# The mixing stage written anew: S5 over four tokens with stacked taps, feature-major q and k, masks and sums by TensorE products, a new order of units

## The reference, cut to what matters

```python
dq, dk, dv, mq, mk, mv, mo, mi, mf, su = split_columns(x @ w_in, IN_WIDTHS)
# differential attention, 4 heads, two maps each, chunk-causal (chunks of 64 tokens)
s = einsum('bqhmd,bkhmd->bhmqk', rope(dq), rope(dk)) * scale
p = softmax(where(allowed, s, -inf)); a = p[:, :, 0] - lam * p[:, :, 1]
a_out = rms_norm(einsum('bhqk,bkhe->bqhe', a, dv), diff_norm_g)
# mLSTM, 4 heads: scores times exp(log_d - m_t), causal, after a 4-tap convolution
qk = silu(causal_conv(concat(mq, mk)))
b_out = sigmoid(mo) * rms_norm(mlstm(q, k, v, gates))
# S5: 16 groups of 16 channels, each a diagonal complex state of 64
x_t = lam_bar * x_(t-1) + b_bar u_t;  y = gelu(Re(C x) + D u);  y = y * sigmoid(y @ glu_w + b)
return concat(a_out, b_out, y) @ w_out
```

## Time and profile before

| what | value |
| --- | --- |
| median of 3 runs | 1377.72 us (1377.54 to 1380.18) |
| profiled execution | 1376.7 us |
| its span, first to last instruction | 1374.9 us |
| mean granted clock of PE | 0.959 of full speed |
| PE busy | 1264.1 us, 92% of the span |
| DVE, ACT, POOL busy | 59%, 42%, 14% |
| data moved | 219.52 MB, mean 160 GB/s |

### The profile page before, as it was taken

How to read it: one execution, slowest core, us unless ns; L and a number is a source line. 1 busy time by engine, 2 the same in 40 slices (tenths; PEclk the granted TensorE clock), 3 DMA queues, 4 the chain that set the end, 5 groups by cost and what they waited for, 6 DMA issues and landing times.

```text
span 1374.9 us, 15895 instructions
## 1 busy us (share of the span) xinstructions
PE 1264.1 (92%) x6568; PEld 1068.6 (78%) x6568; DVE 812.4 (59%) x1130; ACT 578.1 (42%) x656; POOL 192.8 (14%) x181
## 2 busy tenths in 40 slices
...
GB/s 282 236 184 184 184 184 163 144 123 123 31 92 158 128 204 184 184 188 192 192 148 270 186 184 184 184 151 156 92 61 62 139 118 143 152 184 186 190 193 43
DMA packets 155911, 219.52 MB, mean 160 GB/s; under 512 B 6816, under 2 KB 127776, under 8 KB 155840
## 3 DMA queue, kind: packets, MB, share of 16 engines
...
## 4 chain that ended last, share of the span: by engine, by line
PE 65%; issue 16%; DVE 11%; ACT 3%; POOL 2%; DMA 1%; SPq 0%; DVEq 0%; POOLq 0%
PE PS L469 20%; PE PS L470 19%; PE PS L471 19%; DVE WL L1376 3%; ACT WH L1043 1%; PE PS L500 1%; DMA RAW<-in_ffn_w_up 1%; DVE COUT L1560 1%; DVE ZS L1548 1%; PE PS L964 1%; PE PS L988 1%; ACT XH L1043 1%; PE PS L537 1%; POOL RO L1997 1%; ACT PR L1160 1%
## 5 line engine op out<-in xcount | busy, mean ns | idle before, releaser
L1376 DVE TENSOR_TENSOR WL<-RAW,WH 128x2048 fp32r<-128x2048 f32 (+1 forms) x198 | 445.3, 2253 | 272.4 <-ACT WH L1043 272.3
L1043 ACT ACTIVATE WH<-RAW 128x2048 fp32r<-128x2048 f32 (+1 forms) x198 | 370.5, 1877 | 148.4 <-DMA RAW<-in_ffn_w_up 128.5
L469 PE MATMUL PS<-WH,XH 128*128 128x512 f32 x832 | 333.4, 401 | 24.6 <-DVE WL L1376 9.4
L470 PE MATMUL PS<-WL,XH 128*128 128x512 f32 x832 | 327.5, 394 | 0.0
L471 PE MATMUL PS<-WH,XL 128*128 128x512 f32 x832 | 327.0, 393 | 0.0
L469 PEld LDWEIGHTS PS<-WH,XH 128*128 128x128 f32 x832 | 158.2, 190 | 59.0 <-DVE WL L1376 9.9
L471 PEld LDWEIGHTS PS<-WH,XL 128*128 128x128 f32 x832 | 158.2, 190 | 33.8
L470 PEld LDWEIGHTS PS<-WL,XH 128*128 128x128 f32 x832 | 158.4, 190 | 31.0
L469 PE MATMUL PS<-WH,HH 128*128 128x512 f32 x352 | 138.6, 394 | 5.7 <-issue 5.7
L470 PE MATMUL PS<-WL,HH 128*128 128x512 f32 x352 | 137.6, 391 | 0.0
L471 PE MATMUL PS<-WH,HL 128*128 128x512 f32 x352 | 137.6, 391 | 0.0
...
## 6 DMA issues: line engine op xcount, KB each, us to landing
...
```

The costliest lines, as they stand in the source:

```text
L469: nc.tensor.matmul(out_ap, sh, mh, start=first, stop=False)
L470: nc.tensor.matmul(out_ap, sh, ml, start=False, stop=False)
L1043: return nc.scalar.activation(dst, src, ACT.Copy)
L1376: return v.tensor_tensor(dst, full, hi.bitcast(F32), ALU.subtract)
```

## The change

The mixing stage computes the same outputs in another way.

- S5 takes four tokens a step (64 steps). `s5_gather` puts the four taps of u on partitions beside each other, so that `s5_in` is 16 products of 64 columns inside unit `MQ`, `s5_local` 8 and `s5_out` twice 8; `s5_scatter` spreads the result again. DVE makes the states alone (`s5_states`, two calls); POOL has no part in it. In the FFN before it, `scale_c` on POOL is 49 instructions for 25, `s5_turn` is three calls for one, `s5_taps` is 16 products of 128 columns in two halves, and ACT and DVE copy and add more pieces.
- q and k are projected feature-major. RoPE is a copy on ACT, one PE product of 512 columns with a permutation (`swap_halves`, four a layer) and three DVE operations; the turns and POOL's part go.
- The chunk mask is added in PSUM by a product over one row for each score block; the causal mask of the mLSTM decay by products with `tri` in `spread`; ACT then takes exp from PSUM with a bias. `decay_args` and the masking on DVE go.
- Both maps are exponentiated, turned (six turns a head for three) and multiplied by v with a column of ones, which gives the sums; they are combined behind that product. RMS roots go to POOL as a power. One convolution tap moves from DVE to ACT; the gate scaling moves from POOL to DVE.
- The order of units and of all four programs is new. Three fillers of layer 0 stand between the heads, one between `W3` and `W4`.

The core of the diff (the programs of `mix` for PE, then the start of DVE's, without most of their waits):

```diff
-        order += [(l, "DQ", 0), (l, "DQ", 1), (l, "SU", 0), (l, "MQ", 0), (l, "MK", 0), (l, "DK", 0), (l, "DK", 1),
-                  (l, "DV", 0), (l, "DV", 1), (l, "MM", 0), (l, "MM", 1)]
-        order += FILL["mid", l]
-        order += [(l, "W", i) for i in range(5)]
+        order += [(l, "DV", 0), (l, "DV", 1), (l, "DQ", 0), (l, "DK", 0), (l, "SU", 0), (l, "MQ", 0), (l, "MK", 0),
+                  (l, "DQ", 1), (l, "DK", 1), (l, "MM", 0), (l, "MM", 1)]
+        mid = FILL["mid", l]
+        order += mid[0:3] + [(l, "W", i) for i in range(4)] + mid[3:4] + [(l, "W", 4)]
         order += FILL["xattn", l]
...
+def s5_gather(l):
+    pe.wait_ge(ut_ready.sem, ut_ready.at(l, 1))
+    for tap in range(TAPS):
+        r = 32 * tap
+        out_ap = PS[r:r + 32, 5, :].rearrange("p (f j k) -> p j f k", f=2, j=BANDS)
+        for j in range(BANDS):
+            mm = nc.tensor.matmul(out_ap[:, j], ident[:, 32 * j:32 * j + 32],
+                                  UT[:, :, tap * STEPS:tap * STEPS + STEPS], start=True, stop=True)
+    mm.then_inc(u4_done.sem, 1)
...
+def s5_in(l):
+    pe.wait_ge(u4_ready.sem, u4_ready.at(l, 1))
+    for i in range(TILES):
         for part in range(2):
...
+            o = part * 256 + (i % 4) * STEPS
+            mm = nc.tensor.matmul(PS[:, 4 + i // 4, o:o + STEPS], PB[:, i, part, :], U4[:, i, :],
+                                  start=True, stop=True)
+        if i % 4 == 3:
+            mm.then_inc(bu_done.sem, 1)
...
 def s5_local(l):
     pe.wait_ge(km_ready.sem, km_ready.at(l, 1))
...
+    for i in range(TILES):
+        mm = nc.tensor.matmul(PS[:, 2, i * STEPS:i * STEPS + STEPS], KM[:, i, :], U4[:, i, :],
+                              start=(i == 0), stop=False, skip_group_check=True)
+    mm.then_inc(km_used.sem, 1)
...
+def s5_out(l, b):
+    pe.wait_ge(state_ready.sem, state_ready.at(l, b + 1))
+    if b == 0:
         pe.wait_ge(cp_ready.sem, cp_ready.at(l, 1))
...
+    for i in range(4 * b, 4 * b + 4):
+        o = i * STEPS
+        for part in range(2):
+            mm = nc.tensor.matmul(PS[:, 2, o + 1:o + STEPS],
+                                  CQ[:, part, i, 1:TAPS + 1, :].rearrange("p a c -> p (a c)"),
+                                  ZW[:, b, part, (i % 4) * STEPS:(i % 4) * STEPS + STEPS - 1],
+                                  start=False, stop=True, skip_group_check=True)
     mm.then_inc(state_used.sem, 1)
...
+def s5_scatter(l):
+    pe.wait_ge(gelu_done.sem, gelu_done.at(l, 1))
+    g = U4[:, :, :].rearrange("p (f j) k -> p j f k", f=2)
+    for j in range(BANDS):
+        out_ap = PS[32 * j:32 * j + 32, 2, :].rearrange("p (f a k) -> p a f k", f=2, a=TAPS)
+        for tap in range(TAPS):
+            mm = nc.tensor.matmul(out_ap[:, tap], ident[:, 32 * tap:32 * tap + 32], g[:, j],
+                                  start=True, stop=True)
+    mm.then_inc(g4_done.sem, 1)
...
+def swap_halves(l, i):
+    b = (0, 1, 3, 3)[i]
+    pe.wait_ge(swap_in.sem, swap_in.at(l, i + 1))
...
+    nc.tensor.matmul(bank(b), kst[:, K_SWAP:K_SWAP + P], XE[:, :, :].rearrange("p h n -> p (h n)"),
+                     start=True, stop=True).then_inc(swap_done.sem, 1)
...
+def diff_scores(l, h):
+    b = head_bank(h)
+    pe.wait_ge(roped.sem, roped.at(l, 2 if h == 0 else 4))
+    if h >= 2:
+        pe.wait_ge(do_read.sem, do_read.at(l, h - 1))
+    u = h // 2
+    for q0, q1, k1 in ((0, P, P), (P, SEQ, SEQ)):
+        for m in range(2):
+            r = 64 * m
+            nc.tensor.matmul(PS[:, b + m, q0:q0 + k1], DQT[r:r + 64, u, h % 2, q0:q1],
+                             DKT[r:r + 64, u, h % 2, 0:k1], start=True, stop=False,
+                             skip_group_check=True)
+            mm = nc.tensor.matmul(PS[:, b + m, q0 + k1 - 64:q0 + k1], kst[r:r + 1, K_EARLY:K_EARLY + P],
+                                  kst[r:r + 1, K_FAR:K_FAR + 64], start=False, stop=True,
+                                  skip_group_check=True)
+    mm.then_inc(ds_done.sem, 1)
...
 def diff_out(l, h):
+    b = head_bank(h)
     pe.wait_ge(daT_read.sem, daT_read.at(l, h + 1))
...
+    for m in range(2):
+        nc.tensor.matmul(PS[:, b + m, 0:129], AT[:, m, 0:P], DV[:, 0, h, :], start=True, stop=True)
+        nc.tensor.matmul(PS[:, b + m, 129:258], AT[:, m, P:2 * P], DV[:, 0, h, :], start=True, stop=False)
+        mm = nc.tensor.matmul(PS[:, b + m, 129:258], AT[:, m, 2 * P:3 * P], DV[:, 1, h, :],
+                              start=False, stop=True)
+    mm.then_inc(do_done.sem, 1)
...
+def spread(l):
+    pe.wait_ge(cols_read.sem, cols_read.at(l, 1))
+    for i in range(2):
+        for hh in range(2):
+            h = 2 * i + hh
+            pick = ident[0:4, h:h + 1].to_broadcast([4, P])
+            nc.tensor.matmul(PS[:, i, hh * SEQ:hh * SEQ + SEQ], pick, R_MAX, start=True, stop=False,
+                             skip_group_check=True)
+            nc.tensor.matmul(PS[:, i, hh * SEQ:hh * SEQ + P], ident, tri, start=False, stop=True,
+                             skip_group_check=True)
+            nc.tensor.matmul(PS[:, 3, h * P:h * P + P], pick, R_MAX[:, P:SEQ], start=True, stop=False)
+            mm = nc.tensor.matmul(PS[:, 3, h * P:h * P + P], ident, tri, start=False, stop=True)
+        mm.then_inc(mbc_done.sem, 1)
...
+    form_b(UNIT[l, "DQ", 0], 6, XH, XL)
+    form_b_around(UNIT[l, "DK", 0], 7, lambda: swap_halves(l, 0))
+    form_b_around(UNIT[l, "SU", 0], 2, lambda: swap_halves(l, 1))
...
+    s5_gather(l)
...
+    form_b_around(UNIT[l, "MQ", 0], 0, lambda: s5_in(l))
...
+    diff_scores(l, 0)
     s5_local(l)
...
+    form_b(UNIT[l, "MK", 0], 1, XH, XL)
+    diff_turn(l, 0)
...
+    form_b(UNIT[l, "DQ", 1], 4, XH, XL)
+    diff_out(l, 0)
     s5_out(l, 0)
...
+    form_b_around(UNIT[l, "DK", 1], 5, lambda: swap_halves(l, 2))
     s5_out(l, 1)
...
+    form_a_tile(UNIT[l, "MM", 0], 0, 0, XH, XL, 0)
+    swap_halves(l, 3)
+    form_a_tile(UNIT[l, "MM", 0], 0, 0, XH, XL, 1).then_inc(unit_used.sem, 1)
+    diff_scores(l, 1)
+    diff_scores(l, 2)
     cols(l)
...
+    s5_scatter(l)
...
+    form_a_tile(UNIT[l, "MM", 1], 1, 0, XH, XL, 0)
...
+    form_a_tile(UNIT[l, "MM", 1], 1, 0, XH, XL, 1).then_inc(unit_used.sem, 1)
+    diff_turn(l, 1)
...
+    mid(l, 0, 2)
...
+    spread(l)
+    diff_out(l, 1)
+    diff_turn(l, 2)
...
+    mid(l, 1, 3)
+    mlstm_scores(l, 0)
+    mlstm_scores(l, 1)
+    diff_out(l, 2)
+    diff_scores(l, 3)
     mlstm_scores(l, 2)
     mlstm_scores(l, 3)
...
+    fill_read("mid", l, 1)
     mlstm_num(l)
...
+    diff_turn(l, 3)
...
+    turn_cat(l, CATA, 0, 7)
+    mid(l, 2, 6)
+    diff_out(l, 3)
...
     w = UNIT[l, "W", 0]
...
     rows_product(w, [6], CH, CL, True, False)
     rows_product(w + 1, [7], CH, CL, False, False)
...
+    turn_cat(l, CATM, 0, 7)
+    rows_product(w + 2, [0, 1], CH, CL, False, False)
...
+    rows_product(w + 3, [4, 5], CH, CL, False, False)
+    fill_read("mid", l, 2)
+    mid(l, 3, 6)
...
+    turn_cat(l, CATA, 2, 4)
...
+    rows_product(UNIT[l, "W", 4], [2, 3], CH, CL, False, True)
...
+def s5_states(l, b):
...
+    if b == 0:
...
+    else:
...
+    both = PS[:, 4 + b, :].rearrange("p (c n) -> p c n", c=2)
+    z = ZW[:, b]
...
+    v.tensor_tensor(z, both, cos, ALU.mult)
     v.tensor_tensor(ZT[:, :, :], both, sin, ALU.mult).then_inc(bu_read.sem, 1)
...
+    v.tensor_tensor(z[:, 0, :], z[:, 0, :], ZT[:, 1, :], ALU.add)
+    link(v.tensor_tensor(z[:, 1, :], z[:, 1, :], ZT[:, 0, :], ALU.subtract))
+    for part in range(2):
+        ins = v.tensor_tensor_scan(ZS[:, part, :], rad, z[:, part, :], 0.0, ALU.mult, ALU.add)
+    link(ins)
+    v.tensor_tensor(z, ZS[:, :, :], cos, ALU.mult)
+    link(v.tensor_tensor(ZT[:, :, :], ZS[:, :, :], sin, ALU.mult))
+    v.tensor_tensor(z[:, 0, :], z[:, 0, :], ZT[:, 1, :], ALU.subtract)
+    v.tensor_tensor(z[:, 1, :], z[:, 1, :], ZT[:, 0, :], ALU.add).then_inc(state_ready.sem, 1)
...
+def diff_max(l, h):
+    b = head_bank(h)
+    k = 4 * (h % 2)
+    dve.wait_ge(ds_done.sem, ds_done.at(l, h + 1))
+    v.tensor_reduce(SM[:, k:k + 2], PS[:, b:b + 2, 0:P], AX, ALU.max)
+    link(v.tensor_reduce(SM[:, k + 2:k + 4], PS[:, b:b + 2, P:384], AX, ALU.max))
+    v.tensor_scalar(SM[:, 8 + k:12 + k], SM[:, k:k + 4], -0.125, None, ALU.mult).then_inc(ds_max.sem, 1)
...
+def diff_sums(l, h):
+    b = head_bank(h)
+    k = 24 + 4 * (h % 2)
+    dve.wait_ge(do_done.sem, do_done.at(l, h + 1))
+    sums = PS[:, b:b + 2, 0:258].rearrange("p m (t n) -> p m t n", t=TT)[:, :, :, P]
+    link(v.reciprocal(SM[:, k:k + 4].rearrange("p (m t) -> p m t", m=2), sums))
+    link(v.tensor_scalar(SM[:, k + 2:k + 4], SM[:, k + 2:k + 4], CUR[:, R_NLAM:R_NLAM + 1], None, ALU.mult))
+    dve.sem_inc(do_inv.sem, 1)
...
+def diff_combine(l, h):
+    b = head_bank(h)
+    dve.wait_ge(do_first.sem, do_first.at(l, h + 1))
     for t in range(TT):
...
+    split()
+    split()
+    split()
+    rope(l, 0)
+    split()
+    rope(l, 1)
+    split()
+    split()
+    s5_states(l, 0)
+    s5_states(l, 1)
+    diff_max(l, 0)
```

(63 more changed lines are left out.)

1011 lines of the change are left out of this document (411 added, 600 removed).

## The result

The changed kernel takes **1387.83 us** (median of 4 runs, 1386.95 to 1390.62) against 1377.91 for the one before: ratio 1.0072, 95% interval 1.0054 to 1.009. It is slower by 0.7%; the prediction said 1350, 1334 to 1368. The profiled execution took 1390.6 us, its span is 1388.8.

A forecast was written before the change was run, and what follows sets the result against it. PE was taken to bound the kernel, with waits and low clock costing 92.6 us in the mixing stages. Layer 0 17.6 less, layer 1 17.4 less, FFN 7.3 more: 1376.7 becomes 1349.0, median 1350 us, range 1334 to 1368.

The forecast's parts named there:

- The clock I let fall with the waits: Mixing stages: time lost to PE's 1.2 GHz level shrinks in proportion to PE's waits, to 10.5 us from 28.7.
- The price of the masks: Mixing stages: 16 one-row mask products at a turn's 0.15 us, 2.4 us a layer, bounds 0 to 3.8.
- PE's other work: Mixing stages: 31.4 us added and 19.4 removed, 12.0 more a layer at full clock; gather and scatter products at 0.24.
- The waits, 9.5 and 13.5 us: PE's remaining waits in the mixing stages of layers 0 and 1, for 31.0 and 32.9 before.
- the copy `AT` of head 2: Layer 1's mixing stage: PE waits 3.1 us because ACT's split stands ahead of this copy.
- the last RoPE in layer 0: Layer 0's mixing stage: head 1's scores wait 2.3 us for it, behind two fillers' splits in DVE's queue.
- the last decay: mLSTM: the last scores' decay on DVE waits behind a split and the norm, 3.4 us in layer 1, 1.8 in layer 0.
- Head 0's turn: Mixing stages: PE waits 1.7 us in both layers, there at 59.5 while its input is ready at 61.2.
- The FFN, 3.65 us a layer: FFN before the mixing stage: eight more turns and 16 wider products add this much PE work at full clock.
- POOL's preparation: Rival, FFN: POOL's instructions end too late for `s5_taps`, PE stands 32 us in each layer, about 1414; chance 0.08.
- The short products: Rival, mixing stages: they cost by their columns, 0.13 us instead of 0.225, giving 1342; chance 0.03.
- the one on the clock: Rival, mixing stages: waits shrink but the clock stays as bad, 28.7 us lost instead of 10.5, giving 1368; chance 0.13.

The follow-up runs named there:

- masks grouped: Changed kernel with each head's four score products first and its four one-row mask products behind them: 1357.41 us, ratio 0.9841.
- 64 rows: Changed kernel with the mask products reading 64 rows, as their score products do, instead of one: 1354.16 us, ratio 0.9825.
- 64 rows and spread: Changed kernel with mask products over 64 rows and, in `spread`, the 4-row products before the 128-row ones: 1346.74 us, ratio 0.9761.
- the kernel before with one-row products: Kernel before, with a product of one row of zeros behind each of its 16 score products a layer: 1397.44 us, ratio 1.0138.

## Why the prediction was wrong

The profiled execution was to be 1349.0 and was 1390.6, 41.6 us off. By the prediction's own terms:

- **"The clock I let fall with the waits": 3.6 and 6.9 us lost.** The waits did fall, by three quarters, and the clock cost 26.0 and 19.9 us. This is the step that failed, 35 of the 41.6. For the old kernel the traces bear its premise out, though no run varied waits alone: each fall of the clock in its mixing stages came behind a wait. That PE was busy for 57.4 of the 85.3 us at 0.50 says only what it did after the fall. What the step had wrong is that waits are the only source. The new stage brought a second one, products that PE runs without a pause but in alternating heights: seven of nine falls came behind them. With that source taken out the clock cost 13 to 17 us, not far from the 10.5 that the rule gave.
- **The price of the masks, 2.4 us a layer.** The product's own price was right, 0.15 (masks grouped). What was missing is that it stands between two products of another height: it makes both dearer and keeps the two maps from running beside each other, 8.3 and 9.8 us a layer, 0.5 to 0.6 for each mask. The bounds of 0 to 3.8 us a layer were too narrow for the same reason, as they held the product's own cost alone. In `spread`, going to the other height and back eight times was missed likewise, 1.3 to 2.7 us a layer.
- **PE's other work.** Forecast +12.0 a layer, measured +15.3 and +17.2; without masks it is +7.0 and +7.4, where the sum without its 2.4 said +9.6. So the rest came out cheaper than priced. Gather took 2.39 us for 16 products, 0.15 each and not 0.24, and so did scatter where the clock was full (64 rows); that is 2.9 us less a layer. Scatter's 0.24 in the changed kernel was nearly all at 1.2 GHz. `s5_in` was as priced, 0.22.
- **The waits, 9.5 and 13.5 us.** Measured 8.1 and 7.9, in the places named, but for head 0: the copy `AT` of head 2 (3.1 forecast, 2.5), the last RoPE in layer 0 (2.3, 3.5), the last decay (3.4, 1.2). Head 0's turn did not wait, as the low clock had put PE behind DVE. With PE quick again (64 rows and spread) they are 11.6 and 11.8, with 3.1 for `AT`.
- **The FFN, 3.65 us a layer.** From turn to turn PE's work at full clock rose from 201.4 to 205.1 and from 201.0 to 204.3. Right.
- **Next to the stages the clock was left out.** Outside the two mixing stages the low clock cost 12.5 us for 6.3. With the clock's 35, the work's 8.5 and 7.0 less in waits this makes up the 41.6 within 2 us.
- **Rivals.** POOL's preparation was not late. Its first and its last instruction in layer 0's FFN:

```profile
97.53 0.61 POOL L2048 TENSOR_TENSOR LB<-PCB,CUR 128x256 f32<-128x256 f32 x1 [64.62 <-DVE PAR L1981]
...
161.94 0.74 POOL L2070 TENSOR_TENSOR CQ<-CQ,EW 128x256 f32<-128x256 f32 x1 [0.18 <-POOL EW L2069]
```

All 49 end at 162.7, 1.33 us each, 26 us before `s5_taps`. The short products cost 0.22, so they don't go by their moving columns. No rival had PE's own products bring the clock down while it is busy; the one on the clock stopped at the old loss, 1368. That is why the slower side had 0.09.

With the two sources of alternation taken out the kernel runs at 1346.7, 3 us below the forecast. That agreement is partly luck: the work is 4 to 6 us a layer cheaper than summed, the waits are level, and the clock costs 13 to 17 us in the stages for 10.5 and 4 to 6 more than before outside them.

What stays open is the rule of the clock. Taking the alternation out removes most of the new loss, and putting it into the old kernel brings a loss of its own; short products of one height did little or nothing. But nothing here tells what in the alternation does it, the changes themselves or that PE gets less done while it is busy. It isn't the only source beside waits either: behind the grouped `spread` of 64 rows and spread the clock fell at 342.96 us with PE busy all along, and in the kernel before with one-row products it did so at 256.63 and 952.95 us, before any score product of the layer; each time for 3.4 us.
